# Three transformer blocks in one launch: RWKV projections issued after the fourth inversion level, new step rates for differential attention, reworked stage beginnings and a third block on split weights

## The reference, cut to what matters

```
block 1: h = rms_norm(x); p = h @ w_in
         o_rwkv = rwkv7_mix(...)      # 16 heads, a recurrence over time, in chunks of 88 here
         o_diff = diff_attention(...) # 8 heads, two softmaxes, o = (P1 - lam*P2) V
         x += (sig(g0)*(o_rwkv@W) + sig(g1)*(o_diff@W')) @ w_out;  x += relu(rms(x)@W1)^2 @ W2
block 2: LN; gated delta rule, GLA and HGRN2 mixers; three gated branches; w_out; LN1;
         router over 16 experts (top 2), experts of width 256; LN2
block 3: h = rms_norm_3(x); one projection to q, k, v, g of 4 kinds of heads
         forgetting, MoBA, stick-breaking, sliding-window attention; x += concat(o*silu(g)) @ w_out
```

## Time and profile before

| | us |
|---|---|
| three runs | 3927.08, 3900.85, 3912.48; median 3912.48 |
| the profiled execution | 3914.93, its span 3913.0 |
| busy in it | PE 3478.7 (89%), PEld 2787.6, DVE 1604.3, ACT 1237.1, POOL 360.7 |
| mean granted TensorE clock | 0.905 |

### The profile page before, as it was taken

The page is one execution under the profiler, slowest core; times in us unless marked ns, Lnnn a source line. Parts: engine busy times, 40 slices in busy tenths (PEclk is TensorE's granted clock), DMA queues, the critical chain, the costliest instruction groups (busy, mean ns, idle before and its releaser), DMA issues.

```text
span 3913.0 us, 69039 instructions
## 1 busy us (share of the span) xinstructions
PE 3478.7 (89%) x29806; PEld 2787.6 (71%) x29806; DVE 1604.3 (41%) x2836; ACT 1237.1 (32%) x2049; POOL 360.7 (9%) x337
## 2 busy tenths in 40 slices
PE   7888898889788999998788878879899999889998
PEld 6767777778668999996566666657578878355544
DVE  4443544454423343333445355566543344321222
ACT  3223322232322233233434455432222221232341
POOL 4121121112102100000011001110000000000000
PEclk9788897798859999999988889989899999988998
DMA  3001010011004233321112112123133333211111
GB/s 118 21 29 31 21 37 28 23 32 37 21 10 151 86 109 92 92 87 54 55 49 63 46 55 70 55 110 100 46 92 92 92 92 92 67 41 43 33 49 38
DMA packets 72448, 240.70 MB, mean 62 GB/s; under 512 B 8272, under 2 KB 8272, under 8 KB 70736
## 3 DMA queue, kind: packets, MB, share of 16 engines
q1 hardware_dynamic: 65088, 209.17, 17.8%
q0 software_dynamic: 3600, 20.83, 1.4%
q10 hardware_dynamic: 3456, 6.29, 0.4%
HBM read 221.44 MB, written 14.81 MB: 60 GB/s over the span
## 4 chain that ended last, share of the span: by engine, by line
PE 76%; DVE 11%; ACT 9%; issue 3%; DMA 1%; ACTq 0%; DVEq 0%; POOL 0%; SPq 0%; POOLq 0%
PE psum L410 74%; DVE arena L346 5%; ACT arena L331 5%; ACT arena L339 3%; DVE arena L355 2%; PE psum L414 1%; ACT L327 1%; DVE ring L346 1%; DVE arena L350 1%; ACT L331 1%; DMA ring<-in_w 1%; DVE arena L358 0%; DVE arena L367 0%; DVE arena L373 0%; DVE arena L370 0%
## 5 line engine op out<-in xcount | busy, mean ns | idle before, releaser
L410 PE MATMUL psum<-arena,ring 128*128 128x264 f32 (+2 forms) x6248 | 1576.7, 352 | 16.2 <-DVE arena L346 10.6
L410 PE MATMUL psum<-arena,arena 128*128 128x264 f32 (+2 forms) x6160 | 1498.4, 346 | 52.8 <-DVE ring L346 19.8
L410 PE MATMUL psum<-arena 32*32 32x32 f32 (+18 forms) x16376 | 1085.6, 248 | 319.8 <-ACT arena L331 82.4
L410 PEld LDWEIGHTS psum<-arena 32*32 32x32 f32 (+12 forms) x16376 | 771.2, 139 | 623.8 <-issue 277.6
L410 PEld LDWEIGHTS psum<-arena,arena 128*128 128x128 f32 (+1 forms) x6160 | 1013.2, 192 | 218.1 <-issue 52.9
L410 PEld LDWEIGHTS psum<-arena,ring 128*128 128x128 f32 (+1 forms) x6248 | 999.4, 197 | 208.3 <-issue 128.7
L339 ACT ACTIVATE arena<-psum 128x512 f32<-128x512 f32 (+12 forms) x625 | 282.8, 452 | 926.7 <-PE psum L410 817.6
L346 DVE TENSOR_TENSOR ring<-ring,arena 128x1024 fp32r<-128x1024 f32 (+1 forms) x297 | 354.3, 1193 | 515.2 <-ACT arena L339 511.2
L339 ACT ACTIVATE arena<-ring 128x1024 fp32r<-128x1024 f32 (+1 forms) x297 | 304.6, 1026 | 604.7 <-PE psum L410 552.3
L346 DVE TENSOR_TENSOR arena<-arena 128x528 f32<-128x528 f32 (+9 forms) x660 | 327.2, 496 | 245.3 <-ACT arena L331 130.4
L346 DVE TENSOR_TENSOR arena<-arena,psum 88x192 f32<-88x192 f32 (+5 forms) x428 | 193.5, 452 | 536.5 <-PE psum L410 526.2
(11 more groups left out here) (39 smaller groups left out, 840.3 us busy)
## 6 DMA issues: line engine op xcount, KB each, us to landing
ring<-in_w SPq DMA_DIRECT2D x313, 512.0 KB, 3.5
ring<-in_w SPq DMA_DIRECT2D x134, 256.0 KB, 2.6
bg<-arena ACTq DMA_DIRECT2D x24, 256.0 KB, 2.0
arena<-in_x SPq DMA_DIRECT2D x2, 2112.0 KB, 11.4
arena<-bg POOLq DMA_DIRECT2D x1, 3072.0 KB, 17.2
od<-arena POOLq DMA_DIRECT2D x8, 264.0 KB, 2.4
oy<-arena POOLq DMA_DIRECT2D x8, 264.0 KB, 2.4
arena<-oy POOLq DMA_DIRECT2D x2, 1056.0 KB, 7.8
```

The costliest lines, as they stand in the source:

```text
L410: self.last_ins = self.eng.matmul(out, l, r, start=start, stop=stop, skip_group_check=skip)
```

## The change

Block 1, heads, on PE, ACT and DVE alike: `prep(hp + 1)` is queued behind level 16 instead of ahead of level 2, and `pace` is 0.7 up to the levels, 1.0 in them, 0.5 after them. ACT takes the root of `rw_kk` one step earlier. The gate slabs of tile 2 go from `pe_gates` to the end of the heads stage, on POOL's half slabs; `m.sg` has six buffers instead of four, and ACT evaluates these gates ahead of its first high parts for the gates stage.

Block 2: the lora slab and the first mixer slab are taken piece by piece together (`pe_two3`). The branches' first slabs are split by the tail of the mixers' run (`wx.then`), the experts' first ones ahead of LN1. LN1's result is split by ACT (high) and DVE (low) as it is made, and the first two expert slabs follow piece by piece. The router becomes an `mm3` product with 16 output rows behind them, its scores are transposed; DVE does the router's arithmetic after the first expert's product. The sums for the means are added a tile at a time between slabs (`pe_add`).

Block 3: every slab is split by POOL in halves (`m.wz`) and multiplied by `mm3`. The norm's factor `m.rs` is applied when q, k, v, g leave PSUM, by DVE (ACT copied q, k and v before). v is made feature-major and transposed (`turned`, four transposes a tile). The sum of squares, the forget projection and the first q slab go piece by piece. The outputs are split by DVE (`splits`) before `out_lin`.

```diff
@@ heads, PE (the same edits on ACT and DVE)
+PACE = (0.7, 1.0, 0.5)
-    P.beside, P.pace = pe_diff(K, m), 0.7
+    P.beside, P.pace = pe_diff(K, m), PACE[0]
...
-        if hp < 7:
-            P.work.append(prep(hp + 1))
+        P.pace = PACE[1]
         for l in (2, 4, 8, 16):
...
+        P.pace = PACE[2]
+        if hp < 7:
+            P.work.append(prep(hp + 1))
...
         P.drain()
+        P.pace = PACE[0]
...
     P.stage_end("pe", "heads")
+    for g in range(2):
+        gate(g, 2)
@@ act_rwkv
     A.stage_end("act", "heads")
+    for g in range(2):
+        act_gate(K, m, g, 2)
@@ pool_heads
+    while m.wr.lows < len(m.wr.offs):
+        pool_half(K, m.wr)
@@ new
+def pe_two3(K, first, second, xh, xl, of):
+    P, T, todo = K.P, xh[0].shape[1], []
+    for wh, wl, emptied, m in (first, second):
+        todo.append((wh, wl, K.ps[0:m, 512 * P.bank(1, *emptied):][:, 0:T], m))
+    for k in range(8):
+        P.wait_ge(*K.book.at(*of[k]))
+        for n, (wh, wl, out, m) in enumerate(todo):
+            P.mm3([out], wh(k)[:, 0:m], wl(k)[:, 0:m], xh[k], xl[k], k == 0, k == 7)
+            if k == 7:
+                yield n
@@ pe_experts
-    P.wait_ge(*at("normed", "ln1", 7))
-    for j in range(4):
-        for k in range(8):
-            P.mm(ps[:, 512 * b + 16 * j:512 * b + 16 * j + 16], m.x[:, k * T + 128 * j:k * T + 128 * j + 128], K.p["wr"][:, 16 * k:16 * k + 16], k == 0, k == 7)
-    P.did("r_logit")
+    two = [pe_weights(K, m.we, i) + (("e_up" if i else "e_silu", 0, 0), 128) for i in range(2)]
+    for i in pe_two3(K, *two, m.xh_r, m.x_r, [("e_xlow", j) for j in range(8)]):
+        P.did("slab", "experts", i)
+    router()
+    i = 2
     for half in range(2):
         for e in range(8 * half, 8 * half + 8):
-            for f in range(2):
+            for f in range(2) if e else (1,):
...
+                if e == 0:
+                    scores()
+                if e == 1 and f == 0:
+                    shares()
@@ pe_block3
     def glin(off, done, emptied):
-        s, w = P.slab(off, *done)
-        P.wait_ge(*landed(K, s))
         b = P.bank(1, *emptied)
         P.keep(b)
-        for k in range(8):
-            P.mm(bk(b), w[:, k, :], m.h[:, k * T:k * T + T], k == 0, k == 7)
-            if k in (1, 3, 5):
+        for half in range(2):
+            wh, wl, over = pe_half(K, m.wz, off + half * HALF)
+            for k in range(4):
+                kx = 4 * half + k
+                P.mm3([bk(b)], wh(k), wl(k), m.hh_r[kx], m.h_r[kx], kx == 0, kx == 7)
+                if k == 1:
+                    yield
...
+    def turned(t):
+        P.wait_ge(*at("fx_vt", t))
+        b = P.bank(1, "fx_v", t)
+        for J in J4:
+            P.tr(bk(b)[:, J], of_tile(m, t)[0].g[:, J])
+        P.did("fx_vtr", t)
@@ pool_block3
+    for i, taken in enumerate(m.wz.after):
+        while m.wz.lows < taken + 3:
+            pool_half(K, m.wz)
```

More of the change, by code:

```diff
@@ L1048, in pe_rwkv, with gate @@
         P.work.append(f)
+    def gate(g, k):
+        b = P.bank(2, "gate", g, k)
+        P.keep(b, 2)
+        for half in range(2):
+            wh, wl, done = pe_half(K, m.wr, (59 + 3 * k + g) * SLAB + half * HALF)
+            for kk in range(4):
+                pe_terms(K, m, b, wh(kk), wl(kk), 4 * half + kk)
+            P.did(*done)
+            if half:
+                P.also("gate_lin", g, k)
+                P.drop(b, 2)
+            P.advance_both()
     for k in range(2):
         for g in range(2):
[L1051 to L1061, removed]
+            gate(g, k)
     P.drain()
@@ L1959, in memory2 @@
     m.wb = Run(K, "branches", [(w0 + 46 * SLAB + k * (SLAB + 512), 512) for k in range(24)] + run_of(w0 + 81 * SLAB, 8),
-               wh[0:3], [("slab", "mixers", 68)] * 3)
+               wh[1:4] + wh[0:1], [("slab", "mixers", 65 + i) for i in range(4)])
+    m.wx.then = m.wb
     M.top = mark
@@ L2952, in pe_experts @@
                 i += 1
-    K.P.colsum(("mean", "ln2"), ("centred", "ln2", 7), c["ones"], [m.h[:, k * T:(k + 1) * T] for k in range(8)], T, [("e_h", k) for k in range(8)])
+            if half and k == 0:
+                bm = P.bank(1, "centred", "ln2", 7)
+                P.keep(bm)
+            elif half:
+                pe_add(K, bm, m.h[:, (k - 1) * T:k * T], k - 1, "e_h", k - 1)
+    pe_add(K, bm, m.h[:, 7 * T:8 * T], 7, "e_h", 7)
+    P.did("mean", "ln2")
+    P.drop(bm)
     pe_sum8(K, "ln2", m.O, T)
@@ L3496, in qk_tile @@
             yield
+        V.wait_ge(*at("fx_proj", t, n))
+        V.stt(x, bk("fx_" + n, t), 0.125 if n == "q" and not gain else 1.0, m.rs, MUL, MUL, "fx_" + n, t)
         if gain:
@@ L3551, in sticks @@
         d = m.d[1]
-        for _ in range(4):
-            yield from three()
+        yield from qk_tile(t, "q", False)
+        yield from qk_tile(t, "k", False)
+        yield from v_tile(t)
+        yield from gate_tile(t)
         yield
@@ L3612, in dve_block3 @@
     V.ms(m.one4[0:4], 1.0)
[L3613 to L3618 removed]
+    V.wait_ge(*at("root", "n3"))
+    V.wait_ge(*at("fx_flin"))
+    V.tt(m.Z4[0][0:4], out_of(K, 1, T, "fx_forget", m1=4), m.rs[0:4], MUL, "fx_forget")
+    rounds([dense(), local(), tables(), forget(), splits()])
     for k in range(8):
```

447 lines of the change are left out of this document (281 added, 166 removed).

## The result

The changed kernel takes 3940.9 us (median of 10 runs, 3929.2 to 3957.9); before, beside it, 3910.4 (3900.1 to 3927.1). The ratio is 1.0084, with a 95% interval of 1.0064 to 1.0103: slower by 0.8%, where 3857 was forecast. The profiled execution took 3949.17 us, its span is 3947.0, 34.0 more than that of before.

What follows compares the result with a forecast made beforehand. TensorE, busy nearly throughout, was taken as the bound, waiting and slow in the heads' chunks. Gains 28 + 10 + 4 + 7 + 4 + 3 + 0 + 0 = 56 took 3914.93 to 3859, median 3857 us; range 3815 to 3905.

Steps and rivals of the forecast that it cites:

- Heads, "I take 0": Heads stage: savings and costs of the new order and pace sum to -1, taken as 0 us (-40 to +40).
- Chunks +10: Heads, chunk walk: 46.5 us a pair with projections queued there, +1.4 a pair, 10 us slower over seven pairs.
- The leftovers, +17: Attention steps left after pair 7: ten beside the gate slabs cost 10 us, the last four, bare, 7.
- rival D: Heads: chunk clock stays at 0.54, 61 us a chunk walk, +112 for +10, total 3959 us; chance 0.07.
- The signs that I had named for being wrong: Forecast wrong if heads' chunks come above 50 or below 42 us, or block 3's rounds above 450.
- Gate slabs of tile 2, 0: Between heads and gates: moving 11.5 us of PE work into the wait gains nothing, 0 us (-5 to +5).
- Experts +7, branches +4, mixers +3: Block 2 gains from earlier splits and piece-by-piece slabs: 7 us (3 to 13), 4 (2 to 5), 3 (0 to 5).
- Start of block 3, +4: LN2 to first q slab: taking sums, forget projection and q slab piece by piece gains 4 us (0 to 8).
- Rounds, +28: Block 3 rounds: 39 to 54 us of PE work go, 60% of the middle gained, 28 us (8 to 48).
- rival C: Block 3 gets little: POOL's subtractions slow DVE, rounds give 8 us, total 3877 us; chance 0.18.
- Output slabs, +10: Block 3 output: eight converted slabs, less the last split in front, gain 10 us (8 to 12).
- Rival E: The attention's leftovers cost more, or tails add up: 3885 to 3900 us; chance 0.11.

Runs made afterwards that it cites:

- h_old: The changed kernel with the heads stage's old order and pace, and ACT's root of `rw_kk`, put back: 3889.6 us, 0.9946 of before.
- b3_fill: Changed kernel with old heads order and pace and mean banks released late, plus six extra short matmuls per block 3 projection slab: 3916.4 us, 1.0003 of before.
- mid5: `best5` with the next pair's projections queued behind the second inversion level instead of ahead of the first: 3865.6 us, 0.9878 of before.
- best5: Changed kernel with old heads, mean banks released late, reordered expert and gates work, forget gate three rounds later: 3867.7 us, 0.9886 of before.

## Why the prediction was wrong

**Heads, "I take 0"**: measured +50, and this is the step that failed; `h_old` gives 51 back. By its terms: levels -26, measured -21.6 (pairs 0 to 6). Chunks +10, measured +33.6 in these pairs. I took 33 us of work at clock 0.75 and "3 us idle"; there were 31.3 of work, the clock was 0.80, and the idle time was 12.0 a pair, where it had been 10.7. The projections fill some of the steps; the waits of the chunk walk lie between others and stay. I wrote down 11 us of idle time in the earlier trace rows and then let 8 of them vanish without a reason. Pair 7, -2, was -7.8: its chunks found a clock of 0.81 for 0.54 and took 27.8 us for 44.9 with the same work. The other parts of the pairs add 3. The leftovers, +17, were +43: 24 beside the gate slabs for 10, and 19 bare for 7. I had priced the nine steps as work; they are a chain over DVE and ACT, and TensorE stood in front of each. The count (14, for 15) was nearly right. The bound of +40 was too narrow by 10.

The mechanism came closest to rival D: dearer chunks. But D had the low clock in the chunks; it fell in the levels, whose row in pair 7 (26.8 at 0.74) I took as their price: with the changed pace three of pairs 0 to 6 went to 0.5 or 0.6, at the even pace six of seven. From the first level of pair 0 to that of pair 7 the changed kernel has 32 us less of work (attention steps that now stand behind pair 7), but 35 more of loss to the half clock (156 for 121) and 14 more of idle time, so it gets there 17 us later.

The signs that I had named for being wrong said little: chunks of 50 us in the mean for a bound of 50, rounds of 445 for 450. For the stretch behind pair 7, where 43 of the 50 stand, I had named none.

**Gate slabs of tile 2, 0**: +11.7 in front, -9.4 in the gates stage, so +2.3: right.

**Experts +7, branches +4, mixers +3**: from the mixers' start to slab 7 of the experts nothing was gained. The first branch slab's wait went (4.6 us), and branches gave 2.8. The two idles at the router came as forecast (6 and 5; 6.56 and 5.2), and slab 7 would have been 5 us early but for the bank wait, 7.4 us with the slower sum behind it, which I missed because I didn't follow the dealing of banks. The second mixer slab gave nothing: the two slabs take 13.2 us for 11.1 of one, and a gap of 2.5 follows.

**Start of block 3, +4**: from the last expert product to the end of the q slab 4.2 less, with another 7 us bank wait in it; the additions moved into the experts cost 5.2 there (0.74 each).

**Rounds, +28**: 9.4, near rival C's figure of 8. The 39 us of work taken away were the lower end of my 39 to 54, and `b3_fill` shows that nearly all of them were on the path; 23 us of new idle time and 7 of half clock, which I had not priced, took 30 back. So "60%" was no count of anything. **Output slabs, +10**: 9.9.

**The sum**: forecast 56 less; measured 34 more. Heads and gates make 52 of the 90, rounds 19, the two bank waits 15; the rest is the mixers and small pieces. Rival E (3885 to 3900) named leftovers, with a price far below theirs.

## What to carry to other kernels

Idle time inside a chain need not go away because other work is queued beside it (10.7 us a pair became 12.0 here); count which steps are between the waits, or leave the idle time in the sum. Dense work is worth most where its absence would let the clock fall: taken out of a stretch of small matmuls here, it left the levels at 0.50 to 0.60, and the same instructions took 48 us longer in all. One execution a kernel is enough for a difference of 50 us, not for one of 10: look at the same stretch in every trace that has it. When an accumulation is held in a bank over others' slabs, look which bank the next request gets; and when a stage's end carries leftovers, price them as a chain, not as work.

## What the runs showed of the hardware that I had not expected

The cost of the projections' place is not even in it: 2 us less, 9 and 48 us more behind the second, third and fourth level, of which only the 48 is clear of noise. What sets the jump is not settled; the six steps of levels 32 and 64 started at half the clock where the fourth level had no projection, but chunks grew by 30 us too. Nor is it shown what a filler would have to cost to gain anything.

In block 3 the new 23 us of idle time are explained only in part. Some 7 lie in the first 62 us beside the forget gate and hardly went when that was put later. Copies for subtractions took 13 off the idle time of one execution and 4 off the whole. The stretches of 6 us at 76 and 264 us into the rounds stand in every kernel with POOL's subtractions there, copies take 1.4 and 1.6 off them, and no run was aimed at the rest. Nor was one aimed at v's transposes or at DVE's taking q, k and v out of PSUM in ACT's place.

`mid5` (3865.6) and `best5` (3867.7) are the fastest of these kernels: 1.1 to 1.2% under the kernel before, and by the ratios some 2.0% under the changed one. They can't be told apart.
